# Two out projections with the tokens as the stationary operand, and their normalising merged into them

## Chip, cores and metric

The kernel runs on one core of one Trainium2 chip. The metric is the device time of one launch in microseconds. The kernel before was timed three times: 2380.36, 2383.75 and 2380.9 us, median 2380.9.

## What is computed

One step of a two-layer decoder trunk over 1024 prompt tokens and 32 sample tokens (8 sequences of 4), model width 1024. Layer 0 is a pooling mixer of width 2048, layer 1 an attention with forget gates. Each layer ends in an out projection, an RMS norm, a gate and a residual. What the change touches, from the reference:

```python
    y = (mixed * jax.nn.silu(z)) @ out_w                    # layer 0: (tokens, 2048) @ (2048, 1024)
...
            out = (o * jax.nn.silu(zg)) @ b_out_w[j]        # layer 1: (tokens, 1024) @ (1024, 1024)
        x = x + gate * rmsnorm(out, post_g[l])
```

After layer 0 the new x is normalised again, without a weight of its own, and goes in two forms into the next stage: times `kv_g` for keys and values, and times (1 + scale) plus shift for queries and gates.

## The kernel before

All products keep float32 accuracy with two fp32r halves: an operand is rounded to a high part, the rest is the low part, and three products (high x high, high x low, low x high) add up in PSUM. The kernel is a row of stages with a barrier of all engines between them. Four of them matter here. I call the first two the first pair, the last two the second pair.

`stage_out("b", ...)` is layer 0's out projection. The output channels are the stationary operand: weights come in 16 jobs of 8 tiles of 128 x 128 (`stream_weight`, 512 KB each), GpSimd splits them (`split_weights`, L107 and L109), and the moving operand is the whole row of 1056 tokens in three chunks of 352 (`product`, L121). That is 16 x 8 x 3 x 3 = 1152 matmuls of 352 columns. The moving operand is read from DRAM (`mov_b`, 16 rows of tiles) and split once, high on ScalarE (L814), low on VectorE (L841). The result has channels on partitions, so ScalarE copies it out (L830), TensorE turns it back (`TokenRows`, L744), VectorE copies the turned rows into `y_tok` (L754) and ScalarE squares them (L822).

`stage_residual(0, ...)` then takes all nine row tiles (eight of 128 prompt tokens, one of 32 sample tokens): VectorE multiplies by 1/rms and gate (L938), VectorE and GpSimd by turns add x (L874), ScalarE squares (L914), VectorE scales by the new 1/rms (L952). Then `NormedTranspose` turns x on TensorE in 16 rounds of four transposes (L289), VectorE makes the two forms (L327, L329), ScalarE rounds them (L305), VectorE and GpSimd take the low parts (L310).

The second pair, `stage_out("d", ...)` and `stage_residual(1, ...)`, is the same for layer 1 with half as many jobs (8 jobs, 576 matmuls), and ends with the store of the output instead of the turning.

The order on each engine is the program order written in its block; no planner moves anything. SP issues the loads, ScalarE's queue the stores.

## Time and profile before

| what | value |
|---|---|
| median of three runs | 2380.9 us |
| span of the profiled execution | 2378.0 us |
| TensorE busy, share of the span | 2125.1 us, 89% |
| VectorE, ScalarE, GpSimd busy | 906.3, 763.2, 693.5 us |
| mean granted TensorE clock | 0.951 |
| DMA moved | 312.81 MB, mean 132 GB/s |

The profiled execution lasted 2378.0 us from its first to its last instruction; the median of the runs lies 2.9 us above it. A busy TensorE says little by itself, since a matmul's row overlaps the next one's: in a full stretch the distance between starts is what one costs. The granted clock is a share of 2.4 GHz; 0.50 is 1.2 GHz.

### The profile page before, as it was taken

How to read it: one execution, taken by the hardware profiler on the slowest of the kernel's cores; microseconds unless marked ns; L12 is line 12 of the kernel's file. 1: busy time of each engine (PE TensorE's matmuls, PEld its weight loads, DVE VectorE, ACT ScalarE, POOL GpSimd, SP SyncE). 2: the span in 40 equal slices, each digit the busy share in tenths (PEclk: the TensorE clock that was granted, in tenths of full speed). 3: DMA queues.
4: the chain of work that ended last, by engine and by line, in shares of the span. 5: the costliest groups of instructions: out<-in, count | busy, mean ns of one | idle time of the engine just before them, and what ended most of it. 6: DMA issues, size and time to landing. Idle time of an engine off the chain costs nothing. (4 is left out here: it accounts for less than half of the span.)

```text
span 2378.0 us, 33033 instructions
## 1 busy us (share of the span) xinstructions
PE 2125.1 (89%) x12939; PEld 1865.5 (78%) x12939; DVE 906.3 (38%) x1510; ACT 763.2 (32%) x1459; POOL 693.5 (29%) x512
## 2 busy tenths in 40 slices
PE   6969999999799924999999889999999999997692
PEld 1269999999799913999999867778788787876692
DVE  1332333344310066210000166555665655655305
ACT  2111111111212133100001135666666656655332
POOL 0123222333122214222233200444444444441122
PEclk9989999999899955999999889999999999999896
DMA  8621212121421041343333243665656656555404
GB/s 282 220 71 40 83 48 82 49 81 50 175 88 45 18 166 30 110 112 93 84 99 97 87 165 119 227 220 186 213 184 226 213 193 213 187 184 189 143 20 166
DMA packets 231052, 312.81 MB, mean 132 GB/s; under 512 B 39777, under 2 KB 165330, under 8 KB 230779
## 3 DMA queue, kind: packets, MB, share of 16 engines
q1 hardware_dynamic: 199251, 266.13, 34.9%
q10 hardware_dynamic: 31520, 44.50, 5.3%
q8 instruction: 103, 1.69, 0.3%
q14 instruction: 50, 0.41, 0.1%
q0 software_dynamic: 128, 0.07, 0.0%
HBM read 266.09 MB, written 44.57 MB: 131 GB/s over the span
## 5 line engine op out<-in xcount | busy, mean ns | idle before, releaser
L1276 POOL TENSOR_TENSOR Vl<-V,Vh 128x1024 fp32r<-128x1024 f32 x106 | 251.9, 2377 | 2.5 <-ACT Vh L1555 2.5
L121 PE MATMUL ps<-actH,w_hi_a 128*128 128x352 f32 x960 | 210.4, 327 | 3.4 <-DVE w_lo_a L92 3.4
L121 PE MATMUL ps<-actH,w_lo_a 128*128 128x352 f32 x960 | 207.8, 324 | 0.0
L121 PE MATMUL ps<-actL,w_hi_a 128*128 128x352 f32 x960 | 207.4, 324 | 0.0
L121 PE MATMUL ps<-actH,w_hi_c 128*128 128x352 f32 x792 | 173.3, 327 | 20.9 <-DVE w_lo_c L92 20.9
L1694 DVE TENSOR_TENSOR KTl<-ps,KTh 128x512 fp32r<-128x512 f32 x256 | 164.5, 685 | 54.3 <-ACT KTh L1561 52.7
L121 PE MATMUL ps<-actH,w_lo_c 128*128 128x352 f32 x792 | 171.5, 324 | 0.0
L121 PE MATMUL ps<-actL,w_hi_c 128*128 128x352 f32 x792 | 171.4, 325 | 0.0
L121 PEld LDWEIGHTS ps<-actH,w_hi_a 128*128 128x128 f32 x960 | 163.4, 190 | 3.8 <-DVE w_lo_a L92 3.7
L1561 ACT CAST KTh<-ps 128x512 fp32r<-128x512 f32 x256 | 137.4, 588 | 89.5 <-PE ps L1428 86.9
L121 PEld LDWEIGHTS ps<-actH,w_lo_a 128*128 128x128 f32 x960 | 165.5, 189 | 0.0
L121 PEld LDWEIGHTS ps<-actL,w_hi_a 128*128 128x128 f32 x960 | 163.7, 189 | 0.0
L1403 PE MATMUL ps<-kT,qT 64*128 64x512 f32 (+3 forms) x384 | 159.6, 523 | 4.1 <-DMA Vt<-out_dram 1.7
L1428 PEld LDWEIGHTS ps<-ident,K 128*128 128x128 f32 x1024 | 111.6, 142 | 64.5 <-issue 44.2
L121 PEld LDWEIGHTS ps<-actH,w_hi_c 128*128 128x128 f32 x792 | 134.8, 190 | 21.0 <-DVE w_lo_c L92 21.0
L1428 PE MATMUL ps<-ident,K 128*128 128x128 f32 x1024 | 142.3, 283 | 6.8 <-DVE newT L1641 4.6
L107 POOL CAST w_hi_a<-w_raw_a 128x1024 fp32r<-128x1024 f32 (+1 forms) x47 | 43.2, 920 | 333.3 <-PE ps L121 324.4
L1443 PE MATMUL ps<-KTh,qst 128*128 128x256 f32 x512 | 137.1, 306 | 0.0
L121 PEld LDWEIGHTS ps<-actH,w_lo_c 128*128 128x128 f32 x792 | 136.7, 189 | 0.0
L121 PEld LDWEIGHTS ps<-actL,w_hi_c 128*128 128x128 f32 x792 | 135.2, 189 | 0.0
L1443 PE MATMUL ps<-KTl,qst 128*128 128x256 f32 x512 | 124.8, 282 | 0.0
L1555 ACT CAST Vh<-V 128x1024 fp32r<-128x1024 f32 x114 | 118.7, 1041 | 9.0 <-PE ps L1467 8.9
(267 smaller groups left out, 3833.8 us busy)
## 6 DMA issues: line engine op xcount, KB each, us to landing
K<-in_cache_k_dram SPq DMA_DIRECT2D x128, 512.0 KB, 3.3
V<-in_cache_v_dram SPq DMA_DIRECT2D x114, 512.0 KB, 3.4
adaw<-in_ada_w_dram SPq DMA_DIRECT2D x12, 2048.0 KB, 8.5
w_raw_a<-in_a_in_w_dram SPq DMA_DIRECT2D x32, 512.0 KB
g_d<-g ACTq DMA_DIRECT2D x16, 528.0 KB, 2.7
mov_b<-g_d SPq DMA_DIRECT2D x16, 528.0 KB, 5.8
w_raw_b<-in_a_out_w_dram SPq DMA_DIRECT2D x16, 512.0 KB
w_raw_c<-in_kv_w_dram SPq DMA_DIRECT2D x16, 512.0 KB
```

What stands on the lines that cost most here:

```text
L107: pool.tensor_copy(hi, raw).then_inc(w["hi_ready"], 1)
L121: mm = pe.matmul(acc[:, c, 0:CH], wt[:, j % SPL, k, :], act[:, k0 + k, c * CH:(c + 1) * CH], start=first and k == 0 and s == 0, stop=last ...
L1276: eng.tensor_tensor(Vl[:, t % VR], places[t][0], Vh[:, t % VR].bitcast(F32), ALU.subtract).then_inc(s_Vl[t % VR], 1)
L1403: mm = pe.matmul(bank[:, c:e], qT[hs, p % 2, i * P:(i + 1) * P], kT[hs, p % 2, c:e], start=True, stop=True)
L1428: mm = pe.transpose(ps[:, 6 + c // 4, c % 4 * P:(c % 4 + 1) * P], K[:, t % KR, c * P:(c + 1) * P], ident[:, :])
L1443: mm = pe.matmul(out, qst[:, bq % 2, c * P:(c + 1) * P], kt[:, j % 2, c, :], start=False, stop=(c == NP - 1 and kt is KTl))
L1555: act.copy(Vh[:, t % VR], src).then_inc(s_Vh, 1)
L1561: act.copy(KTh[:, s // 2 % 2, 4 * h:4 * h + 4, s % 2 * P:(s % 2 + 1) * P], ps[:, 6 + h, :].rearrange("p (c n) -> p c n", c=4)).then_inc(s_ ...
L1694: dve.tensor_tensor(KTl[:, s // 2 % 2, at[0], at[1]], ps[:, 6 + h, :].rearrange("p (c n) -> p c n", c=4), KTh[:, s // 2 % 2, at[0], at[1]] ...
```

## The change

Both pairs become one stage each. The tokens are now the stationary operand, 128 of them, and the weights move, 512 output channels at a time, so that the result has tokens on partitions at once. `TokenRows`' use for them, `yT`, `ssq` and the two residual stages go.

`stage_pool_out` works in three passes over row tiles (0,1,2), (3,4,5), (6,7,8). A pass has 16 steps, one for each 128 of the 2048 inner channels; each step loads 128 full weight rows (512 KB) and the 384 tokens of the pass (192 KB), and splits both again in each pass. A full row tile takes 6 matmuls of 512 columns in a step (3 products x 2 halves of the channels). The sample tile's 32 tokens stand twice in one stationary tile, high and low part side by side, and take 4; the two results are added after. `post(p, step)` is the work on a finished pass, which ScalarE and VectorE run behind their split of step 16(p+1)+step: copying out and squares at step 1, gate and residual at steps 2 to 4, the second norm at 6, the two forms at 10 to 17; `turn` on TensorE stands behind the next pass's steps 8 to 15. For the last pass no product is left to run beside it.

`stage_attn_out` keeps all weights and tokens split in SBUF (8 steps, one for each 128 inner channels). Row tiles 0, 1 and 2 are done together, channel tile by channel tile as they are split; then the other six in the order 3, 4, 5, 6, 8, 7, each with all 8 steps. ScalarE and VectorE post-process a row tile after it is done.

The high part of the weights is on ScalarE, the low part half on GpSimd and half on VectorE in the first, all on VectorE in the second; both parts of the tokens are on GpSimd. The core of the diff (of removed lines only the calls; the removed functions are printed above):

```diff
--- before.py
+++ after.py
...
+    PASSES = ((0, 1, 2), (3, 4, 5), (6, 7, 8))
+    PW = 3 * P
+    def stage_pool_out():
...
+        wr = a.take("po_w_raw", [P, 2, D])
+        wh = a.take("po_w_hi", [P, 2, D], F32R)
+        wl = a.take("po_w_lo", [P, 2, D], F32R)
+        gr = a.take("po_g_raw", [P, 3, PW])
+        gh = a.take("po_g_hi", [P, 2, PW], F32R)
...
+        y = a.take("po_y", [P, 3, D])
+        xi = a.take("po_x", [P, 3, D])
...
+        def at_step(j):
+            return [(p, j - NK * (p + 1)) for p in range(3) if 0 <= j - NK * (p + 1) < 20]
...
+                def load_x(p):
+                    if p:
+                        sp.wait_ge(s_turn, KD * p)
+                    for t, i in enumerate(PASSES[p]):
+                        sp.dma_start(xi[0:rows_of(i), t, :], x_p[:, i, :] if i < QB else x_s).then_inc(s_x[t], 16)
+                for j in range(JOBS):
+                    p, k = j // NK, j % NK
+                    if j >= 2:
+                        sp.wait_ge(s_wl_pool, j - 1)
+                        sp.wait_ge(s_wl_dve, j - 1)
+                    sp.dma_start(wr[:, j % 2, :], a_out_w[0][k * P:(k + 1) * P, :]).then_inc(s_w[j % 2], 16)
+                    if j >= 3:
+                        sp.wait_ge(s_gl, g_splits(j - 3))
+                    c0 = p * PW
+                    c1 = min(c0 + PW, T)
+                    sp.dma_start(gr[:, j % 3, 0:c1 - c0], g_d[k, :, c0:c1]).then_inc(s_g[j % 3], 16)
...
+                        load_x(0)
+                    if k == 1 and p == 2:
+                        load_x(1)
+                load_x(2)
...
+                for j in range(JOBS):
+                    p, s2, s3 = j // NK, j % 2, j % 3
+                    n = width(p)
+                    pool.wait_ge(s_g[s3], 16 * (j // 3 + 1))
+                    if j >= 2:
+                        pool.wait_ge(s_used, j - 1)
+                    pool.tensor_copy(gh[:, s2, 0:n], gr[:, s3, 0:n]).then_inc(s_gh, 1)
...
+                    pool.wait_ge(s_gh, g_splits(j))
...
+                    pool.tensor_tensor(gl[:, s2, 0:n], gr[:, s3, 0:n], gh[:, s2, 0:n].bitcast(F32),
+                                       ALU.subtract).then_inc(s_gl, 1)
+                    pool.wait_ge(s_wh, j + 1)
+                    pool.tensor_tensor(wl[:, s2, 0:BANK], wr[:, s2, 0:BANK], wh[:, s2, 0:BANK].bitcast(F32),
+                                       ALU.subtract).then_inc(s_wl_pool, 1)
...
+                def turn(p, c):
+                    q = KD * p + c
+                    pe.wait_ge(s_xn, 3 * (p + 1))
+                    if q >= 2:
+                        pe.wait_ge(s_hi, 2 * (q - 1))
+                        pe.wait_ge(s_lo, 2 * (q - 1))
+                    for t, i in enumerate(PASSES[p]):
+                        if i < QB:
+                            mm = pe.transpose(ps[:, 6 + c % 2, t * P:(t + 1) * P], xi[:, t, c * P:(c + 1) * P],
+                                              ident[:, :])
...
+                        j = p * NK + k
+                        s2 = j % 2
+                        pe.wait_ge(s_gl, g_splits(j))
+                        pe.wait_ge(s_wl_pool, j + 1)
+                        pe.wait_ge(s_wl_dve, j + 1)
+                        for t, i in enumerate(PASSES[p]):
+                            if p and k == 0:
+                                pe.wait_ge(s_ev_act, 3 * (p - 1) + t + 1)
+                                pe.wait_ge(s_ev_dve, 3 * (p - 1) + t + 1)
...
+                                at = slice(t * P, (t + 1) * P)
+                                for x, (w, g) in enumerate(((wh, gh), (wh, gl), (wl, gh))):
+                                    for n in range(2):
+                                        mm = pe.matmul(ps[:, 2 * t + n, :], g[:, s2, at], w[:, s2, n * BANK:(n + 1) * BANK],
+                                                       start=k == 0 and x == 0, stop=k == NK - 1 and x == 2)
...
+                        mm.then_inc(s_used, 1)
+                        if p and k >= 8:
+                            turn(p - 1, k - 8)
...
+                for c in range(KD):
+                    turn(2, c)
...
+                    if step == 1:
+                        if p:
+                            act.wait_ge(s_out, 16 * 3 * p)
+                            act.wait_ge(s_xn, 3 * p)
+                        for t, i in enumerate(tiles):
+                            tile_done(act, p, t)
...
+                                act.copy(y[:, t, 0:BANK], ps[:, 2 * t, :]).then_inc(s_ev_act, 1)
...
+                            act.activation(junk[0:r, :], y[0:r, t, :], ACT.Square,
+                                           accum_out=ss[0:r, 0, t:t + 1]).then_inc(s_sq, 1)
...
+                        act.wait_ge(s_var, 2 * p + 1)
+                        act.activation(rstd[:, 0], rstd[:, 0], ACT.Sqrt).then_inc(s_std, 1)
...
+                        act.wait_ge(s_x1, 3 * p + t + 1)
+                        act.dma_start(x1_d[i, 0:r], y[0:r, t, :]).then_inc(s_out, 16)
...
+                        act.activation(junk[0:r, :], y[0:r, t, :], ACT.Square,
+                                       accum_out=ss[0:r, 1, t:t + 1]).then_inc(s_sq2, 1)
...
+                        c, n = step - 10, width(p)
+                        src, cols = ps[:, 6 + c % 2, 0:n], slice(p * PW, p * PW + n)
+                        act.wait_ge(s_turn, KD * p + c + 1)
+                        act.activation(actH[:, c, cols], src, ACT.Copy, scale=kvg[:, c:c + 1]).then_inc(s_hi, 1)
+                        act.activation(actH[:, KD + c, cols], src, ACT.Identity, scale=modulA[:, c, 0:1],
+                                       bias=modulB[:, c, 0:1]).then_inc(s_hi, 1)
...
+                for j in range(JOBS):
+                    s2 = j % 2
+                    act.wait_ge(s_w[s2], 16 * (j // 2 + 1))
+                    if j >= 2:
+                        act.wait_ge(s_used, j - 1)
+                    act.copy(wh[:, s2, :], wr[:, s2, :]).then_inc(s_wh, 1)
+                    for p, step in at_step(j):
+                        post(p, step)
...
+                        if p:
+                            dve.wait_ge(s_out, 16 * 3 * p)
+                        for t, i in enumerate(tiles):
+                            tile_done(dve, p, t)
...
+                                dve.tensor_copy(y[:, t, BANK:D], ps[:, 2 * t + 1, :]).then_inc(s_ev_dve, 1)
...
+                        dve.wait_ge(s_sq, 3 * (p + 1))
+                        dve.tensor_scalar(rstd[:, 0], ss[:, 0], 1.0 / D, EPS, ALU.mult, ALU.add).then_inc(s_var, 1)
+                        dve.wait_ge(s_std, 2 * p + 1)
+                        link(dve, dve.reciprocal(rstd[:, 0], rstd[:, 0]))
...
+                        link(dve, dve.scalar_tensor_tensor(out=y[0:r, t, :], in0=y[0:r, t, :], scalar=rstd[0:r, 0, t:t + 1],
+                                                           in1=G[0:r, q, :], op0=ALU.mult, op1=ALU.mult))
+                        dve.wait_ge(s_x[t], 16 * (p + 1))
+                        dve.tensor_tensor(y[0:r, t, :], y[0:r, t, :], xi[0:r, t, :], ALU.add).then_inc(s_x1, 1)
...
+                            dve.tensor_scalar(xi[0:r, t, :], y[0:r, t, :], rstd[0:r, 1, t:t + 1], None,
+                                              ALU.mult).then_inc(s_xn, 1)
...
+                        dve.tensor_scalar(t1, src, modulA[:, c, 0:1], modulB[:, c, 0:1], ALU.mult,
+                                          ALU.add).then_inc(s_lo, 1)
+                        dve.scalar_tensor_tensor(out=actL[:, c, cols], in0=src, scalar=kvg[:, c:c + 1],
+                                                 in1=actH[:, c, cols].bitcast(F32), op0=ALU.mult,
+                                                 op1=ALU.subtract).then_inc(s_lo, 1)
+                        dve.wait_ge(s_lo, 2 * m + 1)
+                        dve.tensor_tensor(actL[:, KD + c, cols], t1, actH[:, KD + c, cols].bitcast(F32), ALU.subtract)
...
+                    s2 = j % 2
+                    if j < JOBS:
+                        if j >= 2:
+                            dve.wait_ge(s_used, j - 1)
+                        dve.wait_ge(s_wh, j + 1)
+                        dve.tensor_tensor(wl[:, s2, BANK:D], wr[:, s2, BANK:D], wh[:, s2, BANK:D].bitcast(F32),
+                                          ALU.subtract).then_inc(s_wl_dve, 1)
+                    if j == 4:
+                        dve.wait_ge(s_G, 16 * (2 + NB))
+                        link(dve, dve.tensor_tensor(G[:, 0], G[:, 0], postg, ALU.mult))
+                        link(dve, dve.tensor_tensor(G[0:NS, 1], G[0:NS, 1], postg[0:NS, :], ALU.mult))
+                    for p, step in at_step(j):
+                        if (p, step) == (2, 10):
+                            sample_targets()
+                        post(p, step)
...
+    def stage_attn_out():
...
+        ORDER = (0, 1, 2, 3, 4, 5, 6, 8, 7)
...
+                for k in range(KD):
+                    if k >= NRAW:
+                        sp.wait_ge(s_wl, k - NRAW + 1)
+                    sp.dma_start(wr[:, k % NRAW, :], b_out_w[0][k * P:(k + 1) * P, :]).then_inc(s_w[k % NRAW], 16)
+                    if k >= NRAW:
+                        sp.wait_ge(s_gl, 2 * (k - NRAW + 1))
+                    sp.dma_start(gr[:, k % NRAW, :], og_d[k]).then_inc(s_g[k % NRAW], 16)
+                sp.dma_start(G[:, 0, :], gate_d[1, 0:1, :].broadcast_to([P, D])).then_inc(s_G, 16)
+                sp.dma_start(postg[:, :], post_g[1:2, :].broadcast_to([P, D])).then_inc(s_G, 16)
...
+                for n, i in enumerate(ORDER):
+                    if n >= 3:
+                        sp.wait_ge(s_x1, n - 2)
+                    sp.dma_start(xi[0:rows_of(i), n % 3, :], x1_d[i, 0:rows_of(i)]).then_inc(s_x[n % 3], 16)
...
+                for k in range(KD):
+                    raw = gr[:, k % NRAW, :]
+                    pool.wait_ge(s_g[k % NRAW], 16 * (k // NRAW + 1))
+                    pool.tensor_copy(gh[:, k, :], raw[:, 0:SEQ])
+                    pool.tensor_copy(gs[:, k, 0:NS], raw[:, SEQ:T]).then_inc(s_gh, 1)
+                    pool.wait_ge(s_gh, k + 1)
+                    pool.tensor_tensor(gs[:, k, NS:2 * NS], raw[:, SEQ:T], gs[:, k, 0:NS].bitcast(F32),
+                                       ALU.subtract).then_inc(s_gl, 1)
+                    pool.tensor_tensor(gl[:, k, :], raw[:, 0:SEQ], gh[:, k, :].bitcast(F32), ALU.subtract).then_inc(s_gl, 1)
...
+                pe.wait_ge(s_zero, 1)
+                for k in range(KD):
+                    pe.wait_ge(s_wl, k + 1)
+                    pe.wait_ge(s_gl, 2 * (k + 1))
+                    for n in range(3):
+                        row_tile(n, k)
+                for n in range(3, TT):
+                    pe.wait_ge(s_ev_act, n - 2)
+                    pe.wait_ge(s_ev_dve, n - 2)
+                    for k in range(KD):
+                        row_tile(n, k)
...
+                dve.memset(ss[:, :], 1.0).then_inc(s_init, 1)
+                for k in range(KD):
+                    dve.wait_ge(s_wh, k + 1)
+                    dve.tensor_tensor(wl[:, k, :], wr[:, k % NRAW, :], wh[:, k, :].bitcast(F32), ALU.subtract).then_inc(s_wl, 1)
+                dve.wait_ge(s_G, 16 * (2 + NB))
...
+                    dve.wait_ge(s_sq, n + 1)
+                    dve.tensor_scalar(rstd[0:r, n:n + 1], ss[0:r, n:n + 1], 1.0 / D, EPS, ALU.mult, ALU.add).then_inc(s_var, 1)
+                    dve.wait_ge(s_std, n + 1)
+                    link(dve, dve.reciprocal(rstd[0:r, n:n + 1], rstd[0:r, n:n + 1]))
+                    link(dve, dve.scalar_tensor_tensor(out=row, in0=row, scalar=rstd[0:r, n:n + 1], in1=G[0:r, q, :],
+                                                       op0=ALU.mult, op1=ALU.mult))
+                    dve.wait_ge(s_x[n % 3], 16 * (n // 3 + 1))
+                    dve.tensor_tensor(row, row, xi[0:r, n % 3, :], ALU.add).then_inc(s_x1, 1)
...
     end_stage()
     stage_pooling()
     end_stage()
-    arena = Arena(y_at)
-    y_tok = arena.take("y_tok", [P, TT, D])
-    stage_out("b", a_out_w[0], 2, y_tok, arena, actH, actL, g_d)
-    end_stage()
-    arena = Arena(y_at)
-    arena.at += TT * D * 4
-    stage_residual(0, y_tok, arena, lambda i: x_p[:, i, :] if i < QB else x_s,
-                   [(0, kvg, None), (KD, modA[:, 1], modB[:, 1])])
+    stage_pool_out()
     end_stage()
     stage_projections()
     end_stage()
     stage_attention()
     end_stage()
-    arena = Arena(y_at)
-    y2 = arena.take("y2_tok", [P, TT, D])
-    stage_out("d", b_out_w[0], 1, y2, arena, actH, actL, og_d)
-    end_stage()
-    arena = Arena(y_at)
-    arena.at += TT * D * 4
-    stage_residual(1, y2, arena, lambda i: x1_d[i, 0:rows_of(i)], None)
+    stage_attn_out()
     ctx.close()
...
```

Left out: buffers and semaphores, the sample tile's matmuls (`gs` x `wh`, `gs` x `wl`), `sample_targets` (the two forms of the 32 sample tokens: one multiply, 16 narrow operations on 32 columns, and four of 256), `row_tile` (the same six matmuls as above, or four), and ScalarE's part of `stage_attn_out` (copy of half a tile, square, root, store).

## Rows read from the trace of the kernel before

**Rows 1.** Timeline, issues of SP's queue: start us, us, instruction, tiles, count
```profile
625.87 0.37 SPq L78 DMA_DIRECT2D w_raw_b<-in_a_out_w_dram  x1
...
929.57 0.33 SPq L1008 DMA_DIRECT2D fb<-in_f_b_dram  x1
...
2217.21 0.39 SPq L78 DMA_DIRECT2D w_raw_d<-in_b_out_w_dram  x1
```

**Rows 2.** Windows: busy us (count) by engine, granted clock, DMA share, GB/s
```profile
664.00:838.00 174.00, 170.40 (x1063) 168.59 (x1062) 8.84 (x18) 29.14 (x115) 46.34 (x27) 1.00 0.13 37
...
855.00:884.00 29.00, 0.00 (x0) 0.00 (x0) 27.13 (x18) 10.36 (x19) 11.76 (x4) 0.50 0.82 294
...
884.00:929.50 45.50, 17.75 (x72) 12.78 (x72) 42.85 (x86) 20.05 (x33) 26.21 (x16) 0.50 0.00 0
...
2190.00:2210.00 20.00, 12.77 (x44) 7.41 (x44) 12.38 (x11) 9.89 (x10) 0.00 (x0) 1.00 0.57 185
```

**Rows 3.** Timeline of TensorE, first pair's product
```profile
633.55 1.22 PE L121 MATMUL ps<-actH,w_hi_b 128*128 128x352 f32 x3 [12.81 <-DVE actL L841]
...
638.09 1.08 PE L121 MATMUL ps<-actH,w_lo_b 128*128 128x352 f32 x3
...
686.75 0.64 PE L121 MATMUL ps<-actL,w_hi_b 128*128 128x352 f32 x3
...
687.23 0.65 PE L121 MATMUL ps<-actH,w_lo_b 128*128 128x352 f32 x3
...
837.81 0.66 PE L121 MATMUL ps<-actH,w_lo_b 128*128 128x352 f32 x3
...
838.30 1.04 PE L744 MATMUL ps<-ident,yT_b 128*128 128x128 f32 x8
```

**Rows 4.** Line L1467: count, ns min/median/max, first and last start
```profile
L1467 PE MATMUL ps<-Vl,PTd x256: 388/394/628, 1502.1 to 2209.7; 128*128 128x512 f32 x128
```

**Rows 5.** Timeline of TensorE, end of the attention stage
```profile
2194.86 0.63 PE L1467 MATMUL ps<-Vl,PTd 128*128 128x512 f32 x2
```

**Rows 6.** Timeline of GpSimd around the change of stage
```profile
609.22 0.61 POOL L107 CAST w_hi_a<-w_raw_a 128x512 fp32r<-128x512 f32 x1 [9.66 <-PE ps L121]
...
609.91 1.30 POOL L109 TENSOR_TENSOR w_lo_a<-w_raw_a,w_hi_a 128x512 fp32r<-128x512 f32 x1
...
677.82 1.04 POOL L107 CAST w_hi_b<-w_raw_b 128x1024 fp32r<-128x1024 f32 x1 [8.65 <-PE ps L121]
...
678.94 2.40 POOL L109 TENSOR_TENSOR w_lo_b<-w_raw_b,w_hi_b 128x1024 fp32r<-128x1024 f32 x1
```

**Rows 7.** Groups by form, 835 to 960 us: count, busy us, mean ns, idle before
```profile
L938 DVE SCALAR_TENSOR_TENSOR y_tok<-y_tok,rstdr,G 32x1024 f32<-32x1024 f32 x1 | 1.3, 1273 | 0.0
...
L952 DVE TENSOR_SCALAR y_tok<-y_tok,rstdr 128x1024 f32<-128x1024 f32 x8 | 5.4, 749 | 0.0
...
L327 DVE TENSOR_SCALAR tmpr<-ps,modA,modB 128x512 f32<-128x512 f32 x16 | 12.7, 792 | 0.0
...
L914 ACT ACTIVATE ps<-y_tok 128x1024 f32<-128x1024 f32 x8 | 8.2, 1028 | 22.8 <-DVE y_tok L874 13.8 <-POOL y_tok L874 9.0
...
L350 DVE TENSOR_TENSOR tmpr<-ps,modA 128x32 f32<-128x32 f32 x8 | 0.9, 182 | 0.0
```

**Rows 8.** Timeline of VectorE and GpSimd, in the two residual stages
```profile
859.46 4.56 DVE L938 SCALAR_TENSOR_TENSOR y_tok<-y_tok,rstdr,G 128x1024 f32<-128x1024 f32 x2
...
859.76 3.18 POOL L874 TENSOR_TENSOR y_tok<-y_tok,x_in 128x1024 f32<-128x1024 f32 x1 [42.51 <-DMA x_in<-in_x_prompt_dram]
...
2371.25 3.15 POOL L874 TENSOR_TENSOR y_tok<-y_tok,x_in 128x1024 f32<-128x1024 f32 x1 [2.57 <-DMA x_in<-x_d]
...
2372.23 3.24 DVE L874 TENSOR_TENSOR y_tok<-y_tok,x_in 32x1024 f32<-32x1024 f32 x1
```

**Rows 9.** DMA issues: count, KB each, median us to landing
```profile
K<-in_cache_k_dram SPq DMA_DIRECT2D x128, 512.0 KB, 3.3
...
x_in<-in_x_prompt_dram SPq DMA_DIRECT2D x8, 512.0 KB, 6.1
```

## The prediction on record

> **What bounds the kernel now.** I read the page first: TensorE is busy for 89% of the span and its slices fall off in four places, two of which are this change's stages. The queue of SP dates them, because a stage begins with its first load: the first pair runs from 625.87 to 929.57, 303.7 us, the second from 2217.21 to the end of the span at 2378.0, 160.8 us [rows 1]. The windows then tell two kinds of time apart. From 664 to 838 TensorE is busy for 170.4 of 174 us at full clock: there the product sets the pace. From 855 to 884 it does nothing while VectorE is busy for 27.1 of 29 us, and from 884 to 929.5 it works for 17.8 of 45.5 us at half clock while VectorE has 42.9 [rows 2]. So after the last product at 838.5 [rows 3] VectorE's chain sets the end for 91 us, and the second pair ends with some 35 us of the same kind. Third, the timeline of TensorE in the product: three matmuls of 352 columns every 0.486 us, 0.162 us each, and eight transposes in 1.04 us [rows 3].
>
> **Products.** Before: 1152 and 576 matmuls at 0.162. After: steps of 18 matmuls in the two full passes and 16 in the last, (18+18+16) x 16 = 832, and for the second pair 8 x (8x6+4) = 416. What one of 512 columns costs with a new stationary tile is seen once: of two in a row the second starts 0.63-0.39 = 0.24 us after the first [rows 4, 5]. From below, 352 columns take 0.147 at 2.4 GHz and show 0.162; the same surplus of 0.015 on 512 gives 0.228. I take 0.232, bounds 0.228 and 0.240 (-5 to +10 us over 1248). The products become 193.0 and 96.5 us, against 186.6 and 93.3: no gain there. The turning of results goes (9 transposes for each 128 channels, some 1.3 us x 8 per pair), while the 64 transposes of the residual stage stay.
>
> **Start of the first pair.** The first matmul came 7.7 us after the first load [rows 1, 3]; the new chain (512 KB of weights, copy on ScalarE, low parts) has the same length, so 7.7 again. As before the clock is at 1.2 GHz for the first 5.4 us (the row at 638.09 is the last slow one, three matmuls in 1.08 instead of 0.65 [rows 3]); with 0.427 instead of 0.232 a matmul that costs 2.5. Behind the first two steps' loads SP puts gate, norm weight and x of pass 0, about 2.6 MB, 9 us at the 294 GB/s of [rows 2], ahead of step 2: I allow 2 us of waiting, and 1.3 for the two multiplications of G at step 4.
>
> **The split of a step.** Rings of two let the split of step j+2 begin when step j is used up, so it has one step, 18 x 0.232 = 4.18 us. GpSimd's rows at 512 and 1024 columns, 0.61 and 1.04 for a copy and 1.30 and 2.40 for a subtraction [rows 6], give 0.50 and 1.03 at 384 by a straight line; with the weights' half, 1.30, and gaps some 2.95. VectorE's half is 0.6 more (half of 1.27 [rows 7]), and it can't run beside GpSimd: at 859.46 two operations of 1.27 took 4.56 while GpSimd's took 3.18, and at 2372.23 VectorE took 3.24, ending 1.07 after GpSimd's end at 2374.40 [rows 7, 8]. Whoever is second waits for the whole instruction. That makes 3.45 to 3.6 of 4.18: hidden. The post-processing brings more two-input operations to the same lock. Steps 2, 3 and 4 add a gate (1.27) and a residual (same width, 1.2) each: 3.5+2.5 = 6.0 against 4.18. Followed through with the 0.6 of slack, TensorE waits 1.75, 1.3 and 1.2 us, 4.3 a boundary. Step 6 has three scalings of 0.75 [rows 7]. No row shows them beside GpSimd; bounds 0 and 1.3 a boundary. I take 1.3, since 1024 columns in 0.75 are faster than the two-input operations, as if a second way into memory were used. The Trainium skill, SBUF — State Buffer, Who interferes with whom, says the same of both: a VectorE instruction with two SBUF inputs, or in a two-port mode, excludes GpSimd for the whole instruction; for the first the trace agrees (3.24 us above), for the second no row here shows it, and without it the sum would be 2.6 us lower. Steps 10 to 17 add 0.5 of lock only, as the other two operations read PSUM: hidden. Both boundaries with a next pass count: 2 x (4.3+1.3) = 11.2.
>
> **Pass boundaries.** TensorE's first matmul of a pass needs the banks of the last, and both engines stand behind the copy or split of step 17: 1.05 on ScalarE (as the 1.03 of [rows 7]), then VectorE's half, which finds GpSimd in its lock until about 1.7 and ends at 2.3, then a copy of 512 columns: 2.7 us, twice, 5.4. At step 33 SP also waits until pass 0 is turned, and puts 1.5 MB of x ahead of step 34's weights: 2 us more. In the last pass the small sample pieces make GpSimd's chain about 3.95 against 3.7 of products: 1.2 us over the first eight steps. Sixteen turns of three transposes, 0.11 each [rows 3] and a wait of 0.1: 7.
>
> Sum to the last matmul: 7.7+2.5+3.3+193.0+11.2+5.4+2+1.2+7 = 233.3 us (before 212.6).
>
> **Tail of the first pair,** in which nothing is beside the post-processing of pass 2; from the last matmul. VectorE finishes turn 7 of pass 1 at 3.0; the three tiles are copied out at 4.9; the three squares (1.03 and 0.19) end at 7.4; root and reciprocal 8.3; three times gate and residual, 2.5 each, 15.8; last square and root 17.9; three scalings 20.2; the sample's forms, 16 x 0.18 and some 1 us of wider ones, 24.1; eight rounds of two operations at 0.43 (256 columns, by the 0.79 of 512), one of 0.35 and gaps, 1.3 each, 34.5; 1.0 for the barrier, an estimate: 35.5 [rows 7]. The new stage is 268.8 us, 34.9 less.
>
> **Second pair.** A channel tile costs GpSimd 1.04 + 2.40 and two small ones of 32 columns, 0.2 and 0.3, with gaps 4.25; VectorE's 1024 columns of low part add 1.15 in the same lock: 5.35 a step, where TensorE needs 4.18. First data at 5.4 (0.4 of issue, 3.3 to land [rows 9], 0.5 MB more at 294 GB/s), first step ready at 10.8, the eighth at 48.3; the two multiplications of G fall into it, 2.3: 50.6. TensorE ends the first three tiles at 54.8, then (5x48+32) x 0.232 = 63.1 and 0.6 of waits: 118.5. Evacuation, square, root, gate, residual of the last tile 5.5 and its store 2.5 (the last addition ended at 2375.47 [rows 8], the span at 2378.0): 126.5, 34.3 less than 160.8. If GpSimd and VectorE did not exclude each other, the eighth step would be ready at 40 and the end 10 us earlier.
>
> **Sum.** 2378.0 - 34.9 - 34.3 = 2308.8 for a profiled execution; the median of the runs lay 2.9 above the span, so 2312 us.
>
> **Rivals.**
> *The lock costs little* (GpSimd fits into VectorE's gaps, or the waits fall where TensorE has work): without 11.2 and 10, 2291. The stretched rows speak against it [rows 8]; that TensorE's wait is second-hand, through a ring, speaks for it. 0.15.
>
> *The ring of raw weights becomes the bound.* Two buffers: load, copy 1.05, low parts about 1.9, then the next load may start, two steps a round. With a landing of 3.3 [rows 9] and 0.4 of issue the round is 6.7 to 7.2, below the 8.36 of two steps. With 6.1, the median of the x loads where many transfers stand in line [rows 9], it is 9.5: 0.55 a step over some 44 steps, 2336. A step moves 0.7 MB in 4.18 us, 170 GB/s, against 294 shown, so the long landing should be rare; it decides from 4.9 us on. 0.20.
>
> *Slower: the clock.* At 1.2 GHz a 512-column matmul takes at least 0.427, 0.195 more. If 354 of the 1248 run so, the 69 us are gone; if all of the first pair's 832, the kernel takes 162 more, 2474. TensorE fell to 0.50 where it was busy for 17.8 of 45.5 us, but kept 1.00 with 12.8 of 20 busy and an idle stretch at each page [rows 2], and the new stages keep it at over 75%. The Trainium skill, TensorE: Matmul & The Clock Gate, Part 1, lets idle stretches halve the clock; the 0.50 agrees, the 1.00 shows that stretches of this size are not enough. 0.04.
>
> *No difference,* the two tails being hidden work anyway: excluded by the windows, in which TensorE stands still. 0.01.
>
> **Numbers.** The forecast as worked out keeps 0.60; its own range is 2300 to 2326. The 80% range takes in both nearer rivals: 2288 to 2344; the clock and a round of several late loads with slow matmuls are left out. Faster by over 0.2% (4.8 us, about what can be told from no change) 0.95, within 0.01, slower 0.04.
>
> **What would show it.** Right: 512-column matmuls 0.23 apart; 832 and 416 of them; TensorE idle for 2 to 3 us at each of two pass boundaries and over 1 us at the splits of the next three steps, with VectorE or GpSimd instructions stretched to 2 us and more; a tail near 35 us before the projections; in the second pair 5.3 us between channel tiles. Wrong: starts 0.26 or more apart; weight copies on ScalarE waiting for a transfer at most steps; a granted clock of 0.5 inside a pass; or post-processing that falls behind by more than the next pass can hold.

## The result, and the profile after

Before 2380.9 us (2381.6 with a fourth run, taken beside the changed kernel); after **2302.08 us** (median of 4 runs, 2300.84 to 2303.73). The ratio is 0.9663, with a 95% interval of 0.965 to 0.9676: 79 us less. The forecast was 2312 with an own range of 2300 to 2326. The profiled execution has a span of 2298.9 us, 9.9 less than the 2308.8 worked out for it.

SP's queue dates both stages again. Timeline of SP in the changed kernel, as [rows 1]:

```profile
625.54 0.35 SPq L836 DMA_DIRECT2D po_w_raw<-in_a_out_w_dram  x1
...
893.37 0.32 SPq L1288 DMA_DIRECT2D fb<-in_f_b_dram  x1
...
2179.59 0.34 SPq L1120 DMA_DIRECT2D ao_w_raw<-in_b_out_w_dram  x1
```

First stage 893.37 - 625.54 = 267.8 us (303.7 before, 268.8 forecast). Second, to the end of the span, 2298.9 - 2179.59 = 119.3 (160.8 before, 126.5 forecast). What lies between took 1286.2, against 1287.6: nothing was paid back there. So the first stage gave 35.9 us and the second 41.5.

Windows of the changed kernel, columns as in [rows 2]:

```profile
702.00:737.00 35.00, 29.38 (x114) 22.82 (x113) 22.23 (x19) 16.18 (x24) 25.95 (x20) 0.90 0.51 176
737.00:770.00 33.00, 32.80 (x153) 26.76 (x152) 17.09 (x24) 12.06 (x17) 24.15 (x22) 1.00 0.51 167
770.00:815.00 45.00, 35.78 (x149) 28.37 (x148) 26.76 (x31) 21.52 (x33) 32.14 (x40) 0.92 0.55 193
...
2189.00:2229.00 40.00, 35.86 (x145) 27.87 (x146) 15.52 (x11) 8.06 (x10) 34.97 (x29) 0.96 0.58 201
2229.00:2290.00 61.00, 61.00 (x271) 50.51 (x270) 27.51 (x38) 14.84 (x30) 0.00 (x0) 1.00 0.34 108
```

The stretch of [rows 2] in which TensorE did nothing (29 us) is gone. Between the boundaries (737 to 770) and in the last 61 us TensorE is full at full clock. What is left lies in the two windows that hold the pass boundaries, 702 to 737 and 770 to 815, and there the clock column says something that the forecast did not have: 0.90 and 0.92. The timeline of TensorE shows where:

```profile
707.98 1.19 PE L912 MATMUL ps<-po_w_hi,po_g_hi 128*128 128x512 f32 x2 [3.01 <-DVE po_y L1004]
708.97 1.05 PE L912 MATMUL ps<-po_w_hi,po_g_lo 128*128 128x512 f32 x2
709.83 1.05 PE L912 MATMUL ps<-po_w_lo,po_g_hi 128*128 128x512 f32 x2
...
724.54 0.70 PE L912 MATMUL ps<-po_w_hi,po_g_hi 128*128 128x512 f32 x2 [1.16 <-POOL po_w_lo L872]
...
787.53 1.19 PE L912 MATMUL ps<-po_w_hi,po_g_hi 128*128 128x512 f32 x2 [4.30 <-DVE po_y L1004]
...
803.90 0.70 PE L912 MATMUL ps<-po_w_hi,po_g_hi 128*128 128x512 f32 x2 [2.66 <-POOL po_w_lo L872]
...
2239.72 0.62 PE L1161 MATMUL ps<-ao_w_hi,ao_g_hi 128*128 128x512 f32 x2
2240.18 0.62 PE L1161 MATMUL ps<-ao_w_hi,ao_g_lo 128*128 128x512 f32 x2
2240.63 0.61 PE L1161 MATMUL ps<-ao_w_lo,ao_g_hi 128*128 128x512 f32 x2
```

At both boundaries TensorE stands for 3.01 and 4.30 us behind VectorE's copy out of PSUM (L1004), and then two matmuls take 0.86 to 0.99 us instead of the 0.45 of the last three rows, the pace of the 1.2 GHz level. Counted from the first matmul of one step to that of the next, steps 16 and 32 lasted 7.1 and 6.1 us instead of 4.1 and 3.6: 3.0 and 2.5 us of half clock, 5.5 in all. (The expectations below have 7.3 and 6.4, and 3.2 and 2.8, which these rows do not bear out.) What VectorE does ahead of the second copy-out explains why that wait is 1.3 us longer than the first. Timeline of VectorE, changed kernel:

```profile
706.21 1.02 DVE L1072 TENSOR_TENSOR po_w_lo<-po_w_raw,po_w_hi 128x512 fp32r<-128x512 f32 x1 [3.04 <-ACT po_w_hi L982]
707.16 1.87 DVE L1004 COPY po_y<-ps 128x512 f32<-128x512 f32 x3
...
785.12 0.68 DVE L1031 TENSOR_SCALAR po_tmp<-ps,modA,modB 128x384 f32<-128x384 f32 x1
...
786.70 1.88 DVE L1004 COPY po_y<-ps 128x512 f32<-128x512 f32 x3
```

At the first boundary the copy-out (L1004) stands right behind the split; at the second, three operations on the last turned tile (785.12 to 786.78) stand in between.

The lock is seen in stretched rows, as in [rows 8]. Timeline of VectorE and GpSimd, changed kernel:

```profile
716.91 1.74 POOL L872 TENSOR_TENSOR po_w_lo<-po_w_raw,po_w_hi 128x512 fp32r<-128x512 f32 x1
717.43 1.25 DVE L1007 TENSOR_SCALAR po_rstd<-po_ss 128x3 f32<-128x3 f32 x1
...
723.24 2.28 DVE L1013 SCALAR_TENSOR_TENSOR po_y<-po_y,po_rstd,po_G 128x1024 f32<-128x1024 f32 x1
...
738.35 2.33 DVE L1024 TENSOR_SCALAR po_x<-po_y,po_rstd 128x1024 f32<-128x1024 f32 x3
739.20 0.93 POOL L862 CAST po_g_hi<-po_g_raw 128x384 fp32r<-128x384 f32 x1 [1.36 <-PE ps L912]
...
865.65 0.17 DVE L1007 TENSOR_SCALAR po_rstd<-po_ss 128x3 f32<-128x3 f32 x1 [2.14 <-ACT ps L952]
...
2206.64 1.23 DVE L1212 TENSOR_TENSOR ao_w_lo<-ao_w_raw,ao_w_hi 128x1024 fp32r<-128x1024 f32 x1 [3.81 <-ACT ao_w_hi L1182]
2206.72 3.39 POOL L1145 TENSOR_TENSOR ao_g_lo<-ao_g_raw,ao_g_hi 128x1024 fp32r<-128x1024 f32 x1
```

Read the pairs. In the second stage VectorE began 0.08 us ahead, and GpSimd's 2.40 became 3.39: it waited until 2207.87. In the first, GpSimd began at 716.91 and VectorE's operation of three columns, 0.17 us when alone (865.65), took 1.25 and ended at 718.68, when GpSimd's had ended (718.65). I call this exclusion the lock.

### The profile page after: what moved, and what is told of

It reads as the page before. It is cut to its first block and busy times, and to the rows that moved or that the text cites. A ratio compares the mean times of both kernels' runs of the same rounds, so it can differ in the third digit from the quotient of the medians.

```text
span 2298.9 us, 31986 instructions
## 1 busy us (share of the span) xinstructions
PE 2111.2 (92%) x12315; PEld 1800.7 (78%) x12315; DVE 942.2 (41%) x1555; ACT 756.2 (33%) x1267; POOL 781.2 (34%) x654
## 5 line engine op out<-in xcount | busy, mean ns | idle before, releaser
L107 POOL CAST w_hi_c<-w_raw_c 128x1024 fp32r<-128x1024 f32 x32 | 33.2, 1037 | 327.7 <-PE ps L121 277.9
```

Of the source, the lines that this page charges most:

```text
L107: pool.tensor_copy(hi, raw).then_inc(w["hi_ready"], 1)
```

## The experiments

Three of the kernels have the same first stage, and their profiled executions show how far it varies by itself: 267.8, 265.9 and 265.3 us. The third step's load comes sooner or later (idle of 2.32, 1.95 and 1.72 us there), and behind the second boundary the waits over 0.15 us sum to 5.89, 4.21 and 4.65 us; at the first boundary they are the same (3.01, 1.16, 0.73 or 0.75, 0.72 or 0.73). What lies between the two stages is the same code in all kernels, and it too varies, from 1286.0 to 1290.4 us. So a difference of a few us between two medians says little by itself; it is read together with the length of the stage and with its rows, at the first boundary or where they differ by more than this. The numbers side by side (medians of the runs; stages of the one profiled execution, which need not be the median one):

| kernel | median | first stage | between the stages |
|---|---|---|---|
| changed | 2302.08 | 267.8 | 1286.2 |
| copy out first | 2295.28 | 260.5 | 1288.0 |
| + x loads behind the weights | 2296.69 | 262.0 | 1286.0 |
| + squares spread | 2293.05 | 260.4 | 1288.3 |
| the lock, dearer | 2308.77 | 271.1 | 1290.4 |
| the lock, cheaper | 2296.45 | 261.8 | 1286.1 |
| high part on ScalarE, first stage | 2303.6 | 265.6 | 1289.3 |
| high part on ScalarE, second stage | 2295.92 | 265.9 | 1288.8 |
| tail | 2298.42 | 265.0 | 1286.1 |
| first stage alone | 2344.16 | 265.3 | 1288.2 |
| all together | 2276.65 | 249.2 | 1288.3 |

**Copy out first.** In both engines' blocks the copying-out at step 1 of `post` became a function of its own, called ahead of the split of that step:

```diff
+                    if j > 1 and j % NK == 1:
+                        copy_out(j // NK - 1)
                     act.wait_ge(s_w[s2], 16 * (j // 2 + 1))
```

> Edit: in the first pair ScalarE and VectorE copy a finished pass out of PSUM before they take up the split of the second step of the next pass, instead of behind it. Theory: TensorE's idle 3.01 and 4.30 us at the two pass boundaries are that order and nothing else, and the half clock behind them (steps that lasted 7.3 and 6.4 us instead of 4.1 and 3.6) follows from the idle stretch. Then all four go, 3.0+4.3+3.2+2.8 = 13.3 us less the 1 to 2 us that a copy-out of 0.9 us still costs TensorE: median near 2290. Rival 1, the clock falls for another reason: only the idle is saved, near 2295, and the granted clock of the boundary's window stays at 0.90 to 0.92. Rival 2, the split that now comes later makes TensorE wait at the second step of the pass instead: 2300 to 2302.

Measured 2295.28 us (2291.31 to 2296.8, 5 runs), ratio 0.9636 (0.9623 to 0.9649): 6.8 less, somewhat over half of what was expected. Windows, and two rows of TensorE:

```profile
702.00:737.00 35.00, 32.29 (x139) 25.59 (x138) 25.45 (x23) 18.13 (x26) 29.25 (x24) 1.00 0.59 203
...
770.00:815.00 45.00, 37.25 (x159) 29.40 (x158) 28.67 (x35) 21.12 (x32) 34.04 (x43) 0.96 0.59 205
...
721.07 0.70 PE L912 MATMUL ps<-po_w_hi,po_g_hi 128*128 128x512 f32 x2 [1.20 <-DVE po_w_lo L1083]
...
791.75 1.19 PE L912 MATMUL ps<-po_w_hi,po_g_hi 128*128 128x512 f32 x2 [4.73 <-POOL po_w_lo L872]
```

The first boundary went as the theory had it: no idle over 0.15 us until 721.07, and the clock at 1.00. At the second the wait at its first step went too, and another appeared two steps on, of 4.73 us with half clock behind it: of the kind of rival 2, two steps later. The waits over 0.15 us from the second boundary on sum to 8.7 us, as in two of the three kernels with the unchanged first stage (8.5 and 9.0; 10.2 in the changed kernel). So the gain is the first boundary's, and at the second one the wait has moved. I took a load for its cause: SP stood before the x loads of the second pass until step 31 had been turned, and issued the third step's weights behind them. ScalarE copied those at 787.97:

```profile
779.69 1.28 SPq L829 DMA_DIRECT2D po_x<-in_x_prompt_dram  x3
781.06 0.38 SPq L836 DMA_DIRECT2D po_w_raw<-in_a_out_w_dram  x1
...
787.97 1.04 ACT L987 CAST po_w_hi<-po_w_raw 128x1024 fp32r<-128x1024 f32 x1 [0.29 <-DMA po_w_raw<-in_a_out_w_dram]
```

The bracket already speaks against it: ScalarE stood only 0.29 us for the load. Until 787.68 it was busy with the three squares.

**x loads behind the weights,** on top of the last:

```diff
-                    if k == 1 and p == 2:
+                    if k == 2 and p == 2:
                         load_x(1)
```

> Edit: the copy-out first, as in the first experiment, and the x tiles of the second pass are loaded behind the weights of the third step of the last pass instead of ahead of them. In the first experiment's trace SP stood before these x loads until the end of step 31 (779.69), put the third step's weights behind their 1.5 MB (issued at 781.06, copied at 787.97), and TensorE was idle for 4.73 us before 791.75 and at half clock after it. Theory: this order is the whole of that wait. 4.7 us go and 1.7 of half clock, less 1 to 2 for a fourth step's weights that now lie behind x: median near 2290, and the window from 770 to 815 at a clock of 1.00. Rival (the next wait in line, the lock of steps 34 to 36, moves up and eats it): 2294 or more.

Measured 2296.69 us (2292.14 to 2301.38, 5 runs), 0.9643 (0.9627 to 0.966): no gain, and the rival's number; the window from 770 to 815 stayed at a clock of 0.92, not 1.00. But the rival's mechanism was not it either. The weights came in time (issued at 778.36), and ScalarE was busy with the squares, in whose queue their copy stood; ahead of them it had waited 2.10 us for VectorE. Timeline of ScalarE and TensorE, this kernel:

```profile
784.08 1.03 ACT L955 ACTIVATE ps<-po_y 128x1024 f32<-128x1024 f32 x1 [2.10 <-DVE actL L1042]
...
786.57 1.03 ACT L955 ACTIVATE ps<-po_y 128x1024 f32<-128x1024 f32 x1
787.53 0.19 ACT L955 ACTIVATION_READ_ACCUMULATOR ps<-po_y 128x1 f32 x1
787.62 1.03 ACT L987 CAST po_w_hi<-po_w_raw 128x1024 fp32r<-128x1024 f32 x1
...
790.68 1.19 PE L912 MATMUL ps<-po_w_hi,po_g_hi 128*128 128x512 f32 x2 [3.63 <-DVE po_w_lo L1083]
```

**Squares spread,** on top of the last: two of the three squares one step later, and all steps 2 to 6 of the post-processing one later:

```diff
-                    if step == 1:
+                    if step in (1, 2):
                         act.wait_ge(s_ev_act, 3 * (p + 1))
...
-                        for t, i in enumerate(tiles):
+                        for t, i in list(enumerate(tiles))[0:1] if step == 1 else list(enumerate(tiles))[1:3]:
```

> Edit: as in the previous experiment with the x loads behind the weights, and of a finished pass's three squares on ScalarE one stays at the second step of the next pass and two go to the third; everything behind them comes one step later. There, ScalarE's squares ran from 784.08 to 787.7 and the copy of the third step's weights stood behind them (787.62), so that TensorE was idle for 3.63 us before 790.68 and at half clock after it. Theory: ScalarE's queue (three squares of 1.24 us and a copy of 1.05 in a step of 3.62) is the whole of that wait: 3.6 us and 1.7 of half clock go, some 1 us stays, median near 2292, the window from 770 to 815 at 1.00. Rival (the weights that now lie behind the x loads are late by as much): 2295 or more, with a copy on ScalarE waiting for po_w_raw.

Measured 2293.05 us (2290.4 to 2297.8, 5 runs), 0.9625 (0.9612 to 0.9638). The wait of 3.63 became two of 1.19 and 1.67, without a slow matmul behind them. The second is the rival's, a load behind x, issued at 784.43. A third, of 3.15 us and with half clock behind it, stayed as it was (3.18 in the previous kernel), so that the window's clock is 0.96, not the 1.00 expected:

```profile
789.71 0.70 PE L912 MATMUL ps<-po_w_hi,po_g_hi 128*128 128x512 f32 x2 [1.19 <-DVE po_w_lo L1083]
...
791.50 1.05 ACT L987 CAST po_w_hi<-po_w_raw 128x1024 fp32r<-128x1024 f32 x1 [1.56 <-DMA po_w_raw<-in_a_out_w_dram]
...
802.28 1.09 PE L912 MATMUL ps<-po_w_hi,po_g_hi 128*128 128x512 f32 x2 [3.15 <-issue]
```

So at the second boundary waits stood behind one another: the order of the copy-out, then the squares in ScalarE's queue, with the x loads 0.29 us behind them, then waits at the steps that carry gate and residual. The rows show which wait each edit took away, but not that the two later edits gained time: the medians are 2295.28, 2296.69 and 2293.05 with each kernel's runs spread over 5 to 9 us, the first stage lasts 260.5, 262.0 and 260.4 us, and the waits over 0.15 us from the second boundary on sum to 8.7, 7.9 and 7.7.

**The lock, made dearer.** At the third to fifth step of passes 1 and 2 GpSimd also makes VectorE's half of the weights' low part:

```diff
+                    if j - NK in (2, 3, 4) or j - 2 * NK in (2, 3, 4):
+                        pool.wait_ge(s_wl_dve, j)
+                        pool.tensor_tensor(wl[:, s2, BANK:D], wr[:, s2, BANK:D], wh[:, s2, BANK:D].bitcast(F32),
+                                           ALU.subtract).then_inc(s_wl_dve, 1)
```

> Edit: in the first pair, at the third to fifth step of the second and third pass, GpSimd also makes VectorE's half of the weights' low part (512 columns, 1.27 us on GpSimd against 0.60 on VectorE). Theory (one lock for both engines): what the two hold together in a step grows by 0.7 us, and the six waits there (1.16, 0.73, 0.72 and 2.66, 2.25, 0.98 us) grow by 3 to 4 us in sum: median near 2305. Rival (no exclusion, VectorE has only too many instructions in these steps): VectorE is relieved by 0.6 us a step, and the waits shrink, below 2300.

**The lock, made cheaper.** VectorE makes the whole low part at every step, GpSimd none:

```diff
-                    pool.tensor_tensor(wl[:, s2, 0:BANK], wr[:, s2, 0:BANK], wh[:, s2, 0:BANK].bitcast(F32),
-                                       ALU.subtract).then_inc(s_wl_pool, 1)
...
-                        dve.tensor_tensor(wl[:, s2, BANK:D], wr[:, s2, BANK:D], wh[:, s2, BANK:D].bitcast(F32),
+                        dve.tensor_tensor(wl[:, s2, :], wr[:, s2, :], wh[:, s2, :].bitcast(F32),
```

> Edit, the opposite: in the first pair VectorE makes the whole low part of the weights at every step, 1024 columns in about 1.15 us, and GpSimd none (before, 1.27 on GpSimd and 0.60 on VectorE). Theory (lock): what the two hold together falls from 3.4 to 2.7 us a step, and 0.7 us goes from each of the six waits, 3 to 4 in sum: median near 2298. Rival (no exclusion, VectorE overloaded): VectorE's 2.5 us of gate and residual come behind 1.15 instead of 0.6, so the waits grow by 0.5 each: near 2305.

Measured: dearer 2308.77 us (2305.01 to 2310.8, 5 runs), 0.969 (0.9676 to 0.9703); cheaper 2296.45 (2294.86 to 2300.64, 5 runs), 0.9645 (0.9631 to 0.9658). 6.7 more and 5.6 less, both on the theory's side and past its size. Taking work off VectorE slowed the kernel, giving it more sped it up: that is no overloaded VectorE. A GpSimd that is merely too full would give the same two signs. Against it stands that GpSimd has the same work in the steps without post-processing, where TensorE does not wait, and that the rows of both engines are stretched in pairs, as shown above. So it is two engines that exclude each other. Of the first boundary's three waits (1.16, 0.73, 0.72) the dear one made 3.44 and a stretch at half clock; the cheap one left two, 0.23 and 0.27. At the second, the dear one had 2.66, 3.08, 1.12 and 0.98 (7.8 us), the cheap one 1.70, 1.49 and 0.16 (3.4), where the unchanged stage has 4.2 to 5.9. The waits at the copy-out grew by 0.5 us each in the cheap one (3.54 and 4.78), as VectorE's longer split stands ahead of it. TensorE in the dear one:

```profile
725.38 1.19 PE L916 MATMUL ps<-po_w_hi,po_g_hi 128*128 128x512 f32 x2 [3.44 <-POOL po_w_lo L876]
```

**Tokens' high part on ScalarE, first stage:**

```diff
-                    pool.tensor_copy(gh[:, s2, 0:n], gr[:, s3, 0:n]).then_inc(s_gh, 1)
...
+                    act.copy(gh[:, s2, 0:width(j // NK)], gr[:, j % 3, 0:width(j // NK)]).then_inc(s_ghA, 1)
                     act.copy(wh[:, s2, :], wr[:, s2, :]).then_inc(s_wh, 1)
```

> Edit: in the first pair ScalarE makes the tokens' high part (384 columns) ahead of the weights' high part, instead of GpSimd. Theory, the lock between GpSimd and VectorE makes the waits of steps 2 to 4 of a pass (1.16, 0.73, 0.72 us at the first boundary, 2.66, 2.25, 0.98 at the second): GpSimd holds 0.5 to 1.4 us less of each step, and 3 to 5 us of the 8.5 go, median 2297 to 2299. Rival, ScalarE's chain (0.45 more ahead of the weights' copy) delays the low parts by as much as the lock gives back: 2301 to 2303.

Measured 2303.6 us (2302.13 to 2304.59, 5 runs), 0.9676 (0.9663 to 0.9689): the rival. At the first boundary the waits behind steps 2 to 4 of the post-processing did shrink, to 0.92, 0.48 and 0.50, by 0.7 us in sum; at the second they sum to 4.25, within what the unchanged stage has. The copy-out at the second boundary came 1.04 later (5.34 against 4.30), as ScalarE has a longer split ahead of it. So the lock gave back 0.7 us where that can be read, and the queue took 1.0. The whole first stage, 265.6 us, lies within the unchanged one's 265.3 to 267.8: the edit made no difference that these runs can show.

**The same in the second stage** (1024 columns, behind the weights' copy):

```diff
-                    pool.tensor_copy(gh[:, k, :], raw[:, 0:SEQ])
...
                     act.copy(wh[:, k, :], wr[:, k % NRAW, :]).then_inc(s_wh, 1)
+                    act.copy(gh[:, k, :], gr[:, k % NRAW, 0:SEQ]).then_inc(s_ghA, 1)
```

> Edit: in the second pair ScalarE makes the tokens' high part (1024 columns) behind its weights' high part, and GpSimd keeps the low part alone. Theory: GpSimd's chain with VectorE in its lock sets the 5.07 us from one channel tile to the next, so the step falls to 3.9 to 4.2 us, the eighth first matmul comes some 7 x 0.9 = 6.3 us earlier, and the median is near 2296. Rival, the loads set the step (0.5 MB of tokens and 0.5 MB of weights a tile): the step stays at 5.0 and the median at 2302.

Measured 2295.92 us (2294.91 to 2296.2, 4 runs), 0.9643 (0.9629 to 0.9658): 6.2 less, the theory. The stage took 2293.2 - 2180.04 = 113.2 us. TensorE has no wait behind its first matmul, as the window shows (before the edit 35.86 of 40.00):

```profile
2189.00:2229.00 40.00, 40.00 (x171) 32.90 (x171) 23.79 (x15) 17.21 (x20) 25.95 (x21) 0.96 0.61 210
```

So the loads were not the bound: GpSimd's chain with VectorE in its lock was.

**The tail.** The last eight turns of the first stage use four banks instead of two, and GpSimd makes the third operation of a round:

```diff
+                    pool.wait_ge(s_lo, 2 * m + 1)
+                    pool.tensor_tensor(actL[:, KD + c, cols], tmp[:, c % 2, 0:n], actH[:, KD + c, cols].bitcast(F32),
+                                       ALU.subtract).then_inc(s_sub, 1)
```

> Edit: in the last eight turns of the first pair (pass 2) four banks are turned into instead of two, and the last subtraction of each round (256 columns, 0.42 us on VectorE) goes to GpSimd, which has nothing else to do there. Theory: VectorE's own chain of three operations and the wait for ScalarE (0.29 every second round) set the 1.37 us of a round; with two operations left the round falls to ScalarE's 0.93, so the tail is 8 x 0.44 = 3.5 us less, minus 0.5 for GpSimd's last one: median near 2299. Rival (the lock or the hand-over to GpSimd, about 0.75 us an operation, stretches VectorE's operations as much): 2301 to 2303.

Measured 2298.42 us (2298.18 to 2300.27, 5 runs), 0.9649 (0.9635 to 0.9663): 3.7 less. Rounds now start every 0.84 us instead of every 1.34 on average, and from the last matmul to the end of the stage it takes 32.1 us, against 35.4 in the changed kernel and in four others whose tail is the same. The two parts of the edit, banks and GpSimd, were not tried apart. Timeline of VectorE and GpSimd, this kernel:

```profile
884.47 0.54 DVE L1046 TENSOR_SCALAR po_tmp<-ps,modA,modB 128x256 f32<-128x256 f32 x1
884.92 0.48 DVE L1048 SCALAR_TENSOR_TENSOR actL<-ps,kvg,actH 128x256 fp32r<-128x256 f32 x1
885.31 0.54 DVE L1046 TENSOR_SCALAR po_tmp<-ps,modA,modB 128x256 f32<-128x256 f32 x1
...
883.46 6.63 POOL L884 TENSOR_TENSOR actL<-po_tmp,actH 128x256 fp32r<-128x256 f32 x8 [29.10 <-DVE po_tmp L1046]
```

VectorE's two operations read PSUM and at most one operand in SBUF, and kept 0.54 and 0.48 us beside GpSimd's subtraction: no lock here. The Trainium skill, SBUF — State Buffer, Who interferes with whom, has this case too: with at most one SBUF input, outside the two-port modes, VectorE does not contend. The trace agrees, with these durations.

**First stage alone,** the second as in the kernel before:

> Edit: the new first pair with the old second pair, all else as in the changed kernel. If the two savings are independent, as the traces say (267.8 against 303.7 us and 119.3 against 160.8 us), the time is 2302.1 plus 41.5 less what the profile put there: 2343 to 2345. Rival, the first pair's change is paid back in a later stage (clock or transfers): above 2348, with the stages between the pairs longer than 1286 us.

Measured 2344.16 us (2341.02 to 2349.38, 4 runs), 0.9853 (0.9837 to 0.9869): 42.1 above the whole change, where the second stages of the kernel before and of the changed one differ by 41.5. Its profile has 265.3 us for the first stage, 1288.2 between and 160.7 for the old second pair. The two savings are independent.

**All together:** copy-out first, x loads behind the weights, squares spread, low part on VectorE, the tail, and the second stage's high part on ScalarE.

> Edit: all that helped, in one kernel: copy-out first, x loads behind the weights, squares spread, the whole low part of the weights on VectorE, the tail's subtraction on GpSimd with four banks, and in the second pair the tokens' high part on ScalarE. If the parts add up: 2302.1 less about 10 for the boundaries, 3 for what the low part gives beyond them, 3.7 for the tail and 6.2 for the second pair: 2278 to 2281. Rival (VectorE's or ScalarE's queue, now fuller, takes the boundary gain back): 2283 to 2288.

Measured **2276.65 us** (2275.63 to 2280.14, 5 runs), 0.956 (0.9547 to 0.9573): 25.4 below the change and 104 below the kernel before. Windows of its two boundaries, one row of TensorE from the start of the stage, and the first with a wait over 0.15 us behind a boundary:

```profile
702.00:737.00 35.00, 34.47 (x151) 27.60 (x150) 24.60 (x20) 18.51 (x26) 17.70 (x17) 1.00 0.62 212
770.00:815.00 45.00, 40.95 (x180) 32.73 (x179) 32.12 (x36) 22.77 (x34) 26.91 (x42) 1.00 0.65 227
...
648.97 1.19 PE L920 MATMUL ps<-po_w_hi,po_g_hi 128*128 128x512 f32 x2 [4.42 <-DVE po_w_lo L1094]
...
730.24 0.70 PE L920 MATMUL ps<-po_w_hi,po_g_hi 128*128 128x512 f32 x2 [0.23 <-DVE po_w_lo L1094]
```

Both boundaries are at full clock. The row at 648.97 shows what is left, and where: at the third step of the stage, behind the first loads, TensorE waits 4.42 us and comes back at half clock. That wait is 1.7 to 2.3 us long in the unchanged stage and 3.0, 3.7 and 3.4 in the three boundary experiments; no run takes it up. The first stage takes 876.67 - 627.43 = 249.2 us, the second 2278.4 - 2164.99 = 113.4. The parts taken singly give 9.0 (2293.05) + 5.6 + 3.7 + 6.2 = 24.5, so they add up within the spread. The waits over 0.15 us from the second boundary on, 7.7 us with the squares spread and 8.1 with the cheap lock alone, are 4.1 here: it took both.

## Why the prediction was right, step by step

**Bound and mechanism.** Right. VectorE's chain had no product beside it for 91 and 35 us, and all of it but the last pass's went under products. The total alone doesn't tell the forecast from its rival *the lock costs little*: the measured 2302 lies midway between 2312 and 2291, and it is the rows and the edits that show a lock that costs, if less than charged. The ring of raw weights did not bound, as ScalarE's weight copies (L982) waited 103 of 137 us for TensorE to use up a step, and the loads landed in 3.5 us by median, below the 4.9 that would decide. Slow matmuls did appear, and with them one of the forecast's own signs of being wrong, a granted clock of 0.5 inside a pass, but they cost 5.5 us, not the 69 at which the gain is gone.

**Terms of the first stage.**

| term | forecast | measured |
|---|---|---|
| first matmul | 7.7 | 7.85 (633.39) |
| cold start | 2.5 | 2.8 |
| waits of the first steps | 3.3 | 2.8 |
| 832 matmuls | 193.0 | 188.6 (0.2267 each) |
| boundaries, with the x loads | 5.4 + 2 | 3.01 + 4.30 |
| half clock behind them | none | 3.0 + 2.5 |
| lock, with the sample pieces | 11.2 + 1.2 | 2.8 + 5.9 |
| sixteen turns | 7 | 5.9 |
| tail | 35.5 | 35.4 |

The measured rows up to the tail sum to 229.5; the last matmul ended 232.4 after the first load, so 2.9 us lie in smaller gaps than I listed. That the total came within 1.0 us is luck: terms of both signs cancelled, matmuls 4.4, lock waits 3.7 and turns 1.1 too dear, against 5.5 us of half clock and the 2.9 of gaps that were not foreseen.

**The matmul's price.** The step "I take 0.232" was mis-sized: from 2229.30 to 2289.59 a matmul starts every 0.2267 us, just under the lower bound of 0.228 that adding the 352-column surplus gave. It is worth 6.6 us over 1248 matmuls and was the largest error of size.

**The lock.** The mechanism holds, by the stretched pairs and two edits of opposite sign. The sizes at the first boundary came out below those foreseen (1.16, 0.73 and 0.72 instead of 1.75, 1.3 and 1.2; 0.20 instead of 1.3 at step 6), at the second 5.9 against the 6.8 of both terms. That the three scalings exclude GpSimd too, the open point, is shown by the rows at 738.35 and 739.20, 0.93 for a cast of 0.50, and again at 739.34 in the kernel with all edits (1.08). But TensorE waits for it only 0.20 us. The step between is free of such work and may let the split catch up, which the forecast had not counted; no run tests that.

**Pass boundaries.** The step "2.7 us, twice" named the cause rightly (the copy-out behind the split of step 17). The 2 us of x loads were not seen: the second boundary's extra 1.3 us are VectorE's three operations on the last turned tile (785.12), and ScalarE, once past the first steps, waits for weights only at 834.32. The step also missed what an idle stretch of that size does to the clock. The forecast read the clock's fall as a matter of the share of busy time, from the window at 2190 to 2210 of [rows 2], whose idle stretches are short and many.

**Second stage.** 126.5 forecast, 119.3 measured. First step ready after 9.6 us (10.8 forecast), 5.07 a channel tile (5.35), the eighth at 45.1 instead of 50.6: 5.5 of the 7.2 us, and the pace of the matmuls most of the rest. The largest part is GpSimd's own chain. It was charged at 4.25 us a tile, some 0.3 of it for gaps that are not there, and takes 3.8 where nothing holds it. (With the 1.15 of the lock, 4.25 makes 5.40, not the 5.35 that the forecast went on with.) Timeline of GpSimd, changed kernel:

```profile
2210.07 1.03 POOL L1140 CAST ao_g_hi<-ao_g_raw 128x1024 fp32r<-128x1024 f32 x1
...
2213.88 2.04 POOL L1140 CAST ao_g_hi<-ao_g_raw 128x1024 fp32r<-128x1024 f32 x1
```

From 2210.07 to 2213.88 all four operations ran unstretched; VectorE paid instead (2.91 for 1.23 at 2212.11). In the other tiles about 1 us of lock falls on one operation or another, on the subtraction at 2206.72, on the copy at 2213.88, and more in the second and the last. Over the seven tiles, 35.5 us, that leaves 8.8 for the lock with the two multiplications of G, against 10.4 forecast. So of the 5.5 us some 1.2 lie in the start, 2.8 in GpSimd's own operations and 1.5 in the lock.

## What to carry to other kernels

When post-processing is hidden under the next pass, look first at the boundary: what frees the accumulator banks should stand ahead of the next split in both queues. Then look at what else stands in those queues at the next steps; here these were a run of three squares and a large load, and taking them away one by one moved the wait rather than ending it. Where two engines share a lock, work belongs on the one that holds it for the shorter time, even if that engine looks fuller; VectorE's operations that read PSUM and at most one operand in SBUF escaped it here. Removing one wait shows the next at the same place, so follow the rows, and add up the waits of the whole stretch before calling it a gain.

## What the runs showed that I had not expected

**A single idle stretch costs twice.** In the first stage, all kernels taken together, each of the idle stretches of TensorE of 3.15 us and more between two products (up to 5.34) was followed by matmuls at the pace of the 1.2 GHz level. Below that, length alone does not decide: it stayed at full clock after 2.32, 2.66 (twice), 2.70 and once after 3.08 us, and fell after 1.92, 2.63, 2.65, 2.78, 2.83, 2.96, 3.01 (in four profiles) and once 3.08, for the shorter ones some matmuls after it had come back. A fall cost another 1.5 to 3.0 us, and not the same for the same idle stretch: 3.0, 1.7 and 1.5 us behind 3.01 in the three profiles of the unchanged stage. The Trainium skill, TensorE: Matmul & The Clock Gate, Part 1, has idleness halve the clock, and the rows agree.

**The smallest operation waits as long as the largest.** VectorE's scaling of three columns took 1.25 us instead of 0.17 behind GpSimd's subtraction (717.43 and 865.65), and ScalarE's root and all gates of the pass stand behind it.

**Moving work can act through the order of queues alone.** ScalarE's 384-column copy in the first stage took 0.7 us from the waits at the first boundary and added 1.0 at the second copy-out; in the second stage, where no copy-out waits behind it, the same kind of edit gave 6.2 us.
